# Attention with the values stationary, one head in each column half of the matrix engine, and new instruction orders

## The reference

```python
s = jnp.einsum('bshd,bmhd->bhsm', qm.astype(jnp.float32), mk) * (HEAD_DIM ** -0.5)
p = jax.nn.softmax(s, axis=-1)
o = jnp.einsum('bhsm,bmhd->bshd', p, mv)
return o.reshape(B, S, MEM_WIDTH).astype(qm.dtype)
...
o_self = _moba_attention(q, kbh, vbh, kmean).astype(x.dtype)
o_mem = _memory_attention(qm, mem, b_mem_norm[j], b_w_mem_kv[j])
x = x + jnp.concatenate([o_self, o_mem], axis=-1) @ b_w_out[j]
```

## Time and profile before

| | |
|---|---|
| runs | median 915.58 us of 3, from 914.89 to 916.04 |
| profiled execution | 915.4 us (span of its core) |
| PE busy | 907.2 us, 99% of the span |
| PE weight loads busy | 767.8 us, 84% |
| DVE busy | 593.7 us, 65% |
| ACT busy | 490.4 us, 54% |
| POOL busy | 61.3 us, 7% |

### The profile page before, as it was taken

The page is one execution under the profiler, slowest core; times in us unless marked ns, Lnnn a source line. Parts: engine busy times, 40 slices in busy tenths (PEclk is TensorE's granted clock), DMA queues, the critical chain, the costliest instruction groups (busy, mean ns, idle before and its releaser), DMA issues.

```text
span 915.4 us, 13523 instructions
## 1 busy us (share of the span) xinstructions
PE 907.2 (99%) x4824; PEld 767.8 (84%) x4824; DVE 593.7 (65%) x898; ACT 490.4 (54%) x750; POOL 61.3 (7%) x124
## 2 busy tenths in 40 slices
PE   9999999999999999999999999999999999999998
PEld 7778788888888888888888888888788888888887
DVE  4768858555555686746855555667987466555565
ACT  6756666444444566754644444465577464444452
POOL 1102122000000000000200000013130000000000
PEclk9999999999999999999999999999998999999999
DMA  8945137665555453424966555545441447556551
GB/s 297 335 139 183 49 138 236 212 196 183 183 188 193 168 176 103 134 97 149 328 204 197 199 186 184 148 137 197 170 161 43 142 139 230 184 183 188 190 172 47
DMA packets 96885, 159.88 MB, mean 175 GB/s; under 512 B 5969, under 2 KB 37921, under 8 KB 96841
## 3 DMA queue, kind: packets, MB, share of 16 engines
q1 hardware_dynamic: 94240, 155.08, 51.1%
q10 hardware_dynamic: 2568, 4.21, 1.3%
q0 software_dynamic: 32, 0.02, 0.0%
HBM read 158.21 MB, written 3.16 MB: 176 GB/s over the span
## 4 chain that ended last, share of the span: by engine, by line
PE 96%; DVE 2%; ACT 1%; issue 0%; POOL 0%; ACTq 0%; POOLq 0%; DVEq 0%
PE turn L1660 10%; PE proj L1660 9%; PE proj L1604 6%; PE proj L1606 6%; PE proj L1605 6%; PE score L1604 6%; PE score L1605 6%; PE score L1606 6%; PE outp L1604 5%; PE outp L1606 5%; PE outp L1605 5%; PE turn L1664 5%; PE proj L1664 5%; PE outp L1839 3%; PE score L1802 2%; PE turn L1650 2%
## 5 line engine op out<-in xcount | busy, mean ns | idle before, releaser
L1931 DVE TENSOR_TENSOR wlo<-raw,whi 128x2048 fp32r<-128x2048 f32 (+1 forms) x131 | 297.3, 2278 | 171.8 <-ACT whi L1350 132.7
L1350 ACT ACTIVATE whi<-raw 128x2048 fp32r<-128x2048 f32 x64 | 122.7, 1917 | 162.5 <-PE turn L1664 76.2
L1339 ACT ACTIVATE whi<-raw 128x2048 fp32r<-128x2048 f32 (+1 forms) x67 | 126.3, 1896 | 63.3 <-PE proj L1606 16.9
L1604 PE MATMUL proj<-whi,set 128*128 128x512 f32 (+1 forms) x270 | 106.6, 395 | 0.0
L1606 PE MATMUL proj<-whi,set 128*128 128x512 f32 (+1 forms) x270 | 103.8, 384 | 0.0
L1605 PE MATMUL proj<-wlo,set 128*128 128x512 f32 (+1 forms) x270 | 103.5, 383 | 0.0
L1660 PE MATMUL turn<-set,whi 128*128 128x512 f32 x384 | 96.3, 393 | 0.0
L1660 PE MATMUL proj<-set,whi 128*128 128x512 f32 x384 | 95.6, 391 | 0.0
L1604 PE MATMUL score<-whi,set 128*128 128x512 f32 x236 | 93.0, 394 | 0.0
L1605 PE MATMUL score<-wlo,set 128*128 128x512 f32 x236 | 92.1, 390 | 0.0
L1606 PE MATMUL score<-whi,set 128*128 128x512 f32 x236 | 92.0, 390 | 0.0
(11 more groups left out here) (231 smaller groups left out, 1318.5 us busy)
## 6 DMA issues: line engine op xcount, KB each, us to landing
raw<-in_a_w_up SPq DMA_DIRECT2D x32, 512.0 KB, 4.3
raw<-in_a_w_down SPq DMA_DIRECT2D x32, 512.0 KB, 4.5
raw<-in_b_w_up SPq DMA_DIRECT2D x32, 512.0 KB, 4.4
raw<-in_b_w_down SPq DMA_DIRECT2D x32, 512.0 KB, 4.5
raw<-in_w_gate SPq DMA_DIRECT2D x22, 512.0 KB, 4.0
raw<-in_w_up SPq DMA_DIRECT2D x22, 512.0 KB, 5.0
raw<-in_w_down SPq DMA_DIRECT2D x22, 512.0 KB, 4.1
raw<-in_a_w_in SPq DMA_DIRECT2D x20, 512.0 KB, 6.7
```

The lines of the kernel that those rows point to most:

```text
L1339: return act.activation(shaped(whi, u)[:, ks, :], shaped(raw, u)[:, ks, :], ACT.Copy)
L1350: act.activation(shaped(whi, u), shaped(raw, u), ACT.Copy).then_inc(hi_done, 1)
L1604: pe.matmul(out_, hi, wh, start=start, stop=False)
L1931: return dve.tensor_tensor(shaped(wlo, u)[:, ks, :], shaped(raw, u)[:, ks, :], shaped(whi, u)[:, ks, :], ALU.subtract)
```

## The change

For memory, causal and selected heads four things change; differential attention keeps its form.

- `attend` loads the 64 columns of a head's values as the stationary operand and moves the 128 columns of `wT`. Head 0 writes partitions 0 to 63 of a bank and head 1 partitions 64 to 127, so each takes one column half of the array. The output comes out transposed. All of head 0's blocks are issued ahead of head 1's.
- `mix` now multiplies `e` of both heads by 1/sum, since the sums no longer lie along the partitions of the output. `turn_weights` waits for `mix` and no longer for the exponential alone.
- What follows `attend` is an ACT copy into the operand's high part and a DVE subtraction into its low part. The scaling into `o_nat`, and `turn_operand` for these heads, are gone: 28 transposes with seven ACT copies and seven DVE subtractions. In layer A the memory heads' operand has a new buffer, `mem_out`, and one bank of `turn_operand` less; layer B's and the selected heads' halves need none.
- `MOVES` is replaced for PE, DVE and ACT. `KEYS` and `operand` only rename places of buffers.

```diff
 MOVES = {
     "PE": [
-        ("multiply 74", "turn_operand 34"), ("turn_weights 38", "attend 36"), ("turn_weights 37", "attend 35"),
+        ("turn_weights 39", "multiply 74"), ("turn_weights 38", "turn_weights 39"),
...
-        def attend(it, vneed):
+        def attend(it, vneed, lhs=1):
             it.o, it.o_free = o_use()
             it.vneed = vneed
             if it.kind == "diff":
                 count.osq += 1
                 it.osq = count.osq
+            else:
+                count.out += 1
+                k = it.pair + (6 if it.kind == "mem" else 0)
+                it.out, it.turned = count.out, [operand(lhs, part, k)[:, tok(it.t)] for part in range(2)]
             st = add("attend")
...
-                    elif it.kind == "idx":
+                    else:
                         act.wait_ge(o_full, it.o + 1)
-                        act.wait_ge(w_done, it.w)
-                        for c in range(2):
-                            at = it.pair * P + c * DH
-                            ins = act.activation(o_nat[:, it.t, at:at + DH], Ob[it.o % 2][:, c * DH:(c + 1) * DH],
-                                                 ACT.Copy, scale=it.rs[:, c:c + 1])
-                        ins.then_inc(o_evac, 1)
+                        act.activation(it.turned[0], Ob[it.o % 2][:, 0:P], ACT.Copy).then_inc(o_hi, 1)
...
-                    if it.kind == "diff":
-                        pe.wait_ge(w_done, it.w)
-                    else:
-                        pe.wait_ge(exp_done, it.exp + 1)
+                    pe.wait_ge(w_done, it.w)
...
-                            dst = O[:, c * DH:(c + 1) * DH]
                             if it.kind == "diff":
-                                val, dst = v[:, k, it.pair * P:(it.pair + 1) * P], O[:, 0:P]
-                            elif it.kind == "mem":
+                                val = v[:, k, it.pair * P:(it.pair + 1) * P]
+                                ins = pe.matmul(O[:, 0:P], wt, val, start=k == 0, stop=k == nk - 1)
+                                continue
+                            if it.kind == "mem":
                                 val = memkv[:, 1, k * 256 + h * DH:k * 256 + (h + 1) * DH]
...
-                            ins = pe.matmul(dst, wt, val, start=k == 0, stop=k == nk - 1)
+                            ins = pe.matmul(O[HALF[c], 0:P], val, wt, start=k == 0, stop=k == nk - 1)
...
-                    ins = dve.reciprocal(it.rs, it.rs)
+                    behind(dve.reciprocal(it.rs, it.rs))
                     if it.kind == "diff":
...
+                    else:
+                        both = heads_view(e[:, it.buf, 0:2 * it.n], 2)
+                        ins = dve.tensor_tensor(both, both, spread(it.rs, it.n), ALU.mult)
                     ins.then_inc(w_done, 1)
...
-                    if it.kind not in ("diff", "idx"):
-                        dve.wait_ge(o_full, it.o + 1)
-                        dve.wait_ge(w_done, it.w)
-                        dve.tensor_tensor(heads_view(dst, 2), heads_view(O, 2), spread(it.rs, DH), ALU.mult)\
+                    if it.kind != "diff":
+                        dve.wait_ge(o_hi, it.out)
+                        dve.tensor_tensor(it.turned[1], Ob[it.o % 2][:, 0:P], it.turned[0], ALU.subtract)\
                            .then_inc(o_evac, 1)
```

More of the change, by code:

```diff
@@ L58 @@
 STATS = 340
-Q_QB, Q_KA, Q_IK, Q_C = 16, 20, 21, 22
+KEYS = 12
+Q_QB, Q_KA, Q_IK, Q_C = KEYS, KEYS + 4, KEYS + 5, KEYS + 6
 MAX8 = 8
@@ L205, in build @@
     count.decayed, count.w, count.dots, count.rope_read = 0, 0, 0, 0
-    count.up, count.inverse, count.sums = 0, 0, 0
+    count.up, count.inverse, count.sums, count.out = 0, 0, 0, 0
     free = {}
@@ L244, in build @@
         rt = sb("rope_tmp", [P, 2, COLS])
-        qk = sb("qk", [P, 24, TOK])
+        qk = sb("qk", [P, 20, TOK])
+        mem_out = sb("mem_out", [P, 2, 2, TOK], F32R)
         v = sb("v", [P, NT, SELF])
@@ L279, in build @@
         btoep = [memkv[:, :, :].rearrange("p a b -> p (a b)").rearrange("p (h n) -> p h n", h=4),
-                 set_lo[1][:, 0:4, :].bitcast(F32)]
-        fgb = qk[:, 16:20, :].rearrange("p a b -> p (a b)")
+                 mem_out[:, :, :, :].rearrange("p k s n -> p (k s) n").bitcast(F32)]
+        MEM_OUT = 2
+        fgb = qk[:, KEYS:KEYS + 4, :].rearrange("p a b -> p (a b)")
         gn = zq[:, 0, :, :]
@@ L292, in build @@
         biasvec = e[0:8, 1, :]
-        grow = [qk[0:len(group) * KT, 23 - i, 0:P] for i, group in enumerate((GAINS[:FIRST], GAINS[FIRST:]))]
+        grow = [qk[0:len(group) * KT, KEYS + 7 - i, 0:P] for i, group in enumerate((GAINS[:FIRST], GAINS[FIRST:]))]
         ncol = [0]
@@ L329, in build @@
         o_full = sem("o_full")
+        o_hi = sem("o_hi")
         osq_done = sem("osq_done")
@@ L393, in t_use, with operand, turn_operand @@
             return n
-        def turn_operand(src, half, gains, ready, set_free, cols=None):
-            use = [t_use(), t_use()]
-            for b in range(2):
+        def operand(lhs, part, k):
+            if lhs == MEM_OUT:
+                return mem_out[:, k - 6, part, :] if k >= 6 else sets[1][:, k, part, :]
+            return sets[lhs][:, k, part, :]
+        def turn_operand(src, half, gains, ready, set_free, banks=2):
+            use = [t_use() for _ in range(banks)]
+            for b in range(banks):
                 st = add("turn_operand")
@@ L401, in turn_operand @@
                 st.b, st.use, st.hi = b, use, count.hi
-            count.hi += 2
+            count.hi += banks
             return use
@@ L649, in build @@
         mul_chunk_half(vm, 0, 0, x1)
-        qk_pieces = lambda a: pairs(0, a, 2, SCALE) + pairs(2, 16 + a, 2)
+        qk_pieces = lambda a: pairs(0, a, 2, SCALE) + pairs(2, KEYS + a, 2)
         mul_chunk_half(vm, 1, 0, x1)
@@ L658, in diff_item @@
         def diff_item(h, t):
-            return scores("diff", h, t, h, qk[:, 16 + h, :], h_use[h // 2])
+            return scores("diff", h, t, h, qk[:, KEYS + h, :], h_use[h // 2])
         h_use = [turn_heads(zq[:, 1], [0, 1, 2, 3], qk_pieces(0), rope_ready(r0.rope))[-1]]
@@ L686, in build @@
         mul_chunk_half(qk2, 0, 0, x1, mixed=m[2:4])
-        attend(m[0], memV); attend(m[1], memV); turn_weights(m[2]); turn_weights(m[3])
+        attend(m[0], memV, MEM_OUT); attend(m[1], memV, MEM_OUT); turn_weights(m[2]); turn_weights(m[3])
         mul_chunk_half(qk2, 1, 0, x1)
@@ L691, in build @@
         zfree[1] = h_use[1] + 1
-        attend(m[2], memV); attend(m[3], memV)
+        attend(m[2], memV, MEM_OUT); attend(m[3], memV, MEM_OUT)
         d += [diff_item(2, 0), diff_item(2, 1)]
@@ L720, in build, with finish_attention @@
         memB_chunk = ev.chunk
-        def finish_attention(w, items, o_half, last_qset_unit, oset, gain, vneed, around):
+        def finish_attention(w, items, o_half, last_qset_unit, gain, vneed, around):
             ua, ub, uc, ud = out_units(w)
-            o1 = turn_operand(o_nat, 0, [(None, oset, 0)], (o_evac, o_half), 2 * last_qset_unit + 2)[-1]
+            diff = items[0].kind == "diff"
+            o1, lhs = (o_evac, o_half), 1
+            if diff:
+                o1, lhs = turn_operand(o_nat, 0, [(None, 1, 0)], o1, 2 * last_qset_unit + 2)[-1], MEM_OUT
             attend(items[0], vneed); attend(items[1], vneed)
             turn_weights(items[2]); turn_weights(items[3])
-            if items[0].kind == "diff":
+            if diff:
                 norm(items[0:2])
@@ L734, in last_items, with last_turned @@
                 o_all = attend(items[3], vneed)
-                if items[0].kind == "diff":
+                if diff:
                     norm(items[2:4])
                 return o_all, done
-            o_all, done = multiply_around(last_items, ua, oset, 0, o1, "P", True, False)
+            def last_turned():
+                if not diff:
+                    return o_evac, o_all
+                return turn_operand(o_nat, 1, [(None, 1, UK)], (o_evac, o_all), 0, banks=1)[-1]
+            o_all, done = multiply_around(last_items, ua, lhs, 0, o1, "P", True, False)
             split(ua + AHEAD)
-            o2 = multiply_around(lambda: turn_operand(o_nat, 1, [(None, oset, UK)], (o_evac, o_all), 0)[-1],
-                                 ub, oset, 0, o1, "S", True, False)
-            return out_tail(ub, (uc, oset, UK, o2), (ud, oset, UK, o2), 1 - oset, gain), done
+            o2 = multiply_around(last_turned, ub, lhs, 0, o1, "S", True, False)
+            return out_tail(ub, (uc, lhs, UK, o2), (ud, lhs, UK, o2), 0, gain), done
         def out_tail(u, third, fourth, xset, gain):
@@ L757, in memory_keys @@
             return turn_heads(zq[:, 1], [0, 1], mem_keys, chunk_ready(memB_chunk))[-1]
-        (uses_a, r), mkB = finish_attention(A["a_w_out"][0], d[8:12], o8, memB[1], 1, g_at("a_norm_mlp"), vneed,
+        (uses_a, r), mkB = finish_attention(A["a_w_out"][0], d[8:12], o8, memB[1], g_at("a_norm_mlp"), vneed,
```

(25 more changed lines are left out.)

## The result

| | before | after |
|---|---|---|
| median of 21 runs, us | 915.96 (914.85 to 917.29) | 917.52 (916.07 to 918.62) |
| ratio to before | 1 | 1.0017, 95% interval 1.0010 to 1.0023 |
| span of the profiled execution, us | 915.4 | 915.3 |
| PE busy, us | 907.2 | 900.7 |
| DVE busy, us | 593.7 | 607.9 |

The account below looks back on a forecast made before the run. PE was taken as the bound, with 96% of the chain: -3.1 (transposes) -2.7 (attends with switches) +1.1 +0.7 +0 -0.8 = -4.8 us on 915.4, 910.6, plus 0.2 for the median: 910.8 us, range 906.5 to 918.2.

Parts of the forecast that it names:

- the price of the scaling on DVE: Multiplying by 1/sum in mix was priced from the nearest rows at 16.7 us of DVE time.
- a wait at the index ahead of u100: PE waits there for the index's transposes, moved ahead of unit u100: +0.7 us, bounds 0 and 5.0.
- rival 4: The index comes no earlier, so PE waits 5.0 instead of 0.7 us at u100: 915.1 us, chance 0.07.
- Rival 1: In the attends the column halves take turns instead of overlapping: 918.0 us, slower by 0.3%, chance 0.18.
- 46 or 59 steps: Attends on PE: 46 steps (10.0 us) if halves go independently, 59 (12.9 us, taken) if strictly in program order.
- rival 2: In the attends each column half has its own queue, 10.0 us in place of 12.9: 907.9 us, chance 0.20.
- switches from 1.6 to 6.5 us: Bounds on PE's cost of changing to half the array and back around 18 attend groups; 4.5 us was taken.
- Most of it lies beside the products of a unit: Claim that most added DVE and ACT work, about +14 us on DVE, hides beside PE's products except in three places.
- the idle spots that get work: Two idle spots of PE, at 9.97 and 114.78 us, get work from the new orders: 0.4 each, -0.8 us.
- Rival 3: Normalisation comes onto the path: all six causal pairs, not one, show their 1.1 us, +5.5: 916.3 us, chance 0.10.
- a round less later: Selected heads: one more selection round ahead of the first masked maximum, one less before the second mask; counted 0, bounds 1.5 us either way.
- one pair's scaling: Causal stretch between u59 and u60: one of three pairs shows its scaling ahead of the attends, +1.1 us, range 0 to 3.3.

Follow-up runs that it names:

- old_form: Changed kernel with attends of memory, causal and selected heads in their old form (transposed weights stationary, whole array), all else as changed; 922.68 us, 1.0068.
- alternate: Changed kernel with the two heads of an attend issued in turn, block by block; 917.56 us, 1.0011.
- third_two: third_old plus the two moves of two_moves (last statistics, one round of the selection); 915.08 us, 0.9984 to the kernel before.
- third_old: Changed kernel with 80 steps of the third block, up to the selected heads' scores, in the old order on PE, DVE and ACT; 916.24 us, 1.0002.
- third_no_scale: third_two without the multiplication by 1/sum in mix, outputs not normalised; 911.32 us, 0.9948 to the kernel before.
- banks: Changed kernel with four steps moved on DVE and ACT (a weight rest later, subtractions and copies behind attends earlier) to free banks earlier; 917.94 us, 1.0014.
- all_fixes: Changed kernel with the moves of two_moves and banks together; 916.94 us, 1.0004.
- two_moves: Changed kernel with last statistics ahead of the next weight's copy (ACT) and one selection round behind the first masked maximum (DVE); 916.85 us, 1.0001.
- no_scale: Changed kernel without the multiplication of the exponentials by 1/sum in mix, outputs not normalised; 915.53 us, 0.9987.

## Why the prediction was wrong

**What was right.** 28 transposes fewer, passes in pairs, the price of the scaling on DVE, and a wait at the index ahead of u100: forecast 0.7, it was 1.2, far from the 5.0 of rival 4. Rival 1, the one that ended slower, is refuted by rows and by old_form: the halves do not take turns. The kernel came out slower by another way.

**Attends: a size that was off, to the good side.** Forecast 46 or 59 steps with 59 taken, -2.7 us; old_form measures 4.7, and alternate shows that the halves go by themselves. This was rival 2, to which I gave 0.20; with its 46 steps the sum is -5.6. What a switch of the mode costs for column halves was not measured by itself, apart from the 0.17 us on the way out. The bounds of the forecast itself were mis-added: switches from 1.6 to 6.5 us give 907.9 to 912.8, not 908.5 to 913.5.

**"Most of it lies beside the products of a unit": the step that failed.** I let +14 us on DVE count in three places only and came to +1.1, +0.7 and 0, less 0.8 for the idle spots that get work, +1.0 in all. Take the measured parts: -3.1 for transposes (counted, not measured alone) and -4.7 for attends leave +9.4 us behind the measured +1.6, where I had +1.0. PE's waits show 5.9 of them (11.1 against 5.2 in the lists). The rest was not settled; it can lie in the error of the 4.7 and in the clock, since the kernel before ran a quarter of its executions wholly at full speed, which neither profile shows. The experiments name two thirds of the 9.4:

- The scaling ahead of `turn_weights` costs 2.7 us in the changed kernel and 3.3 in third_two. Rival 3 had that mechanism at 5.5 us above the forecast, in the causal stretch alone; the price was spread over more places, the memory heads and the clock at the selected heads among them, and the causal stretch has only 0.6 of it.
- The new orders cost 3.0 us: 1.4 in the third block up to the selected heads, the rest in the last statistics and the selection (third_two against third_old). Between the two profiles, which have the same mean clock, it is 2.0, and in the lists of waits 1.7. For these places I had counted +0.7, all of it at the index. The wait for the last statistics, 1.6 instead of 0.6, I did not look for at all: the square sum of the last tile moved behind the copy of a weight on ACT, which is no part of the attention.
- Some 3 us are left: third_no_scale has -4.8, where -3.1 and -4.7 would give -7.8. Its list of waits accounts for 2.5 of them: it holds 7.7 us where before had 5.2, with 2.5 at the selected heads (1.5 before) and smaller ones. banks tried the waits for a bank and found that each came back at the next step of the chain; which step sets that chain was not settled.

**The selected heads.** I set the round of the selection that was moved against a round less later, and counted 0. The wait grew from 1.5 to 2.6 us, and the round is what was added: in the changed kernel it starts at 686.18 and the masked maximum behind it at 687.16, 0.98 us later, and with the round back the wait is 1.6 (all_fixes). My upper bound, as much again, was nearly the answer. A second thing of the same size hides this in two_moves: where POOL's part of the group gain begins ahead of DVE's, DVE's first operation takes 1.66 us instead of 0.69. The runs have all four cases: 1.6 with neither (all_fixes), 2.6 with the round (the changed kernel), 2.5 with the slow operation (two_moves, third_two) and 3.5 to 3.7 with both (third_old, no_scale). Which engine begins first turned on 0.01 to 0.55 us in these runs; the forecast had no term for it, and it was seen in the rows and not tried by itself. The half-speed stretch behind these heads did not grow: both profiles have a mean clock of 0.996.

**The causal stretch.** The forecast was one pair's scaling, 1.1 us. PE's rows between units u59 and u60, first, waits and end:

```profile
390.48 0.38 PE L1896 MATMUL turn<-ident,e 128*128 128x128 f32 x2
...
393.93 0.93 PE L1886 MATMUL score<-qk 64*128 64x128 f32 x8 [0.66 <-DVE stat L2237]
...
397.75 0.44 PE L1921 MATMUL outp<-wT,v 128*64 128x128 f32 x4 [0.64 <-issue]
...
400.86 0.48 PE L1688 MATMUL proj<-whi,set 128*128 128x512 f32 x1
```

The stretch takes 10.4 us where it took 11.5, with waits of 0.66 and 0.64 in these rows and of 0.27 and 0.22 between them, 1.8 in all. That is near the forecast in size, but mostly not for its reason: without the scaling the stretch takes 399.25 - 389.46 = 9.8 us, so the scaling is worth 0.6 there, and no_scale still has waits of 0.64 and 0.58 there.

**The base.** I set the sum against the profile's span and added 0.2 for the median. That mixes two things: the span leaves out 1.7 us of the time, and the profiled execution was itself about 1.1 us longer than the median. The two errors nearly cancel, by luck: 916.0 - 4.8 = 911.2, where I wrote 910.8. As a ratio the forecast was 0.9948, which is by chance what third_no_scale measured.

## What to carry to other kernels

Putting two heads into the two column halves pays on PE as its passes say, here 4.7 us, but it moves the softmax's normalisation ahead of the transposes, onto the chain from scores to attend; price that by leaving it out in one run, not by asking whether its engine is busy. Where steps are ordered by a table for each engine, compare every place of the new order with the old one, also where the operations did not change, since a wait of 1 us can come in anywhere; and when one is put back, put it back on all engines that take part. Where a wait does not change although its supposed cause is gone, read the rows ahead of it: here an operation that began a little behind another engine's took the cause's place. A forecast from a profile is a ratio to that execution, not to the median of the runs.

## What the runs showed of the hardware

**Column halves start by themselves.** With all of head 0's blocks issued ahead of head 1's, sixteen passes still took 1.05 us, and 1.02 with the heads in turn. Two of them start within the first 0.05 us, where passes of one half are 0.11 apart (PE's timeline of the kernel after, 89.05 to 89.10 us):

```profile
89.07 0.34 PE L1921 MATMUL outp<-wT,memkv 128*64 128x128 f32 x2 [0.70 <-issue]
```

The Trainium skill (TensorE: Matmul & The Clock Gate, Part 3: Packing small matmuls) has matmuls begin strictly in program order; by that the first form would have needed five steps of 0.218 us and a way out, 1.26 us, and the measurement decides against it for halves of the array.

**POOL slows beside DVE.** In the kernel after, rows of POOL and DVE at 85 us:

```profile
85.24 2.79 POOL L1341 TENSOR_TENSOR newton<-newton 128x2 f32<-128x2 f32 x1
88.12 0.19 POOL L1342 TENSOR_SCALAR newton<-newton 128x2 f32<-128x2 f32 x1
...
85.69 2.28 DVE L2013 TENSOR_TENSOR wlo<-raw,whi 128x2048 fp32r<-128x2048 f32 x1
88.62 0.61 DVE L2264 SCALAR_TENSOR_TENSOR o_nat<-outp,stat,subln 128x128 f32<-128x128 f32 x2 [0.64 <-POOL stat L1343]
```

An operation on two columns took 2.79 us while DVE formed a weight rest, and 0.19 us right after it. The norm that frees the bank waited for it, and behind the bank the attend at 89.07 us. So a weight rest on DVE can hold up a chain on POOL that has nothing to do with it; this was seen in the rows and not tried by itself.
